# The second group's front in bunches of pieces behind each quartet of sums, instead of one piece behind every fetch

## The reference, cut to what matters

```python
h = rms_norm(x, norm1_gain) * (1 + scale1) + shift1
z = h @ w_in                                   # q, k, v, conv inputs, merge gates
y_att = attend(q, k, v) @ w_o_att              # banded attention, 8 heads x 64
y_conv = (cb * conv_y) @ w_o_conv              # short convolution
mixed = (sigmoid(ga) * y_att + sigmoid(gb) * y_conv) @ w_o
x = x + gate1 * mixed
h2 = rms_norm(x, norm2_gain) * (1 + scale2) + shift2
# PEER: for each frame, 8 heads pick the top 16 of 128 x 128 experts
u = take(expert_u, idx); act = gelu(einsum("thkd,td->thk", u, h2))
out = einsum("thk,thkd->td", softmax(top) * act, take(expert_v, idx))
x = x + gate2 * out
```

## Time and profile before

| | |
|---|---|
| Time, median of 3 runs | 2077.7 us (2077.1 to 2078.39) |
| The profiled execution | 2079.57 us, its span 2077.4 us |
| PE busy over the span | 1690.4 us (81%) |
| DVE busy | 1221.6 us (59%) |
| ACT busy | 724.9 us (35%) |
| Indirect gathers | 604.02 MB, 71.3% of the time of the 16 DMA engines |
| Mean granted TensorE clock | 0.957 of full speed |

### The profile page before, as it was taken

One profiled execution on the slowest core, in us unless ns is written; L12 is line 12 of the kernel. 1 busy time (PEld: TensorE's weight loads), 2 busy tenths in 40 slices (PEclk: granted clock), 3 DMA queues, 4 the chain that ended last, 5 costly groups with the idle time before them and its releaser, 6 DMA issues.

```text
span 2077.4 us, 22509 instructions
## 1 busy us (share of the span) xinstructions
PE 1690.4 (81%) x7500; PEld 771.4 (37%) x7500; DVE 1221.6 (59%) x3212; ACT 724.9 (35%) x2231; POOL 607.4 (29%) x584
## 2 busy tenths in 40 slices
PE   6999997669978799989967777777777777777776
PEld 3864896435445455445522121121121121121111
DVE  3334116866565454447867777777677675555554
ACT  3125103442475223232343333333333343333332
POOL 0000001332322223222254434434444434333331
PEclk8999999779977999999999999999999999999999
DMA  9546514889965799967799999999999999999995
GB/s 400 212 173 255 221 52 167 341 336 385 358 235 199 315 400 370 421 254 276 269 373 422 421 421 422 421 421 421 421 421 421 422 421 422 421 422 421 421 421 240
DMA packets 102467, 718.50 MB, mean 346 GB/s; under 512 B 13584, under 2 KB 13584, under 8 KB 15696
## 3 DMA queue, kind: packets, MB, share of 16 engines
q0 software_dynamic: 82944, 604.02, 71.3%
q1 hardware_dynamic: 18544, 110.69, 13.6%
q10 hardware_dynamic: 864, 2.36, 0.3%
HBM read 712.30 MB, written 4.73 MB: 345 GB/s over the span
## 4 chain that ended last, share of the span: by engine, by line
DMA 41%; PE 30%; DVE 14%; issue 10%; ACT 4%; POOL 1%; SPq 0%; DVEq 0%; POOLq 0%; ACTq 0%
DMA ring<-in_expert_uv_dram,uidx 40%; PE ps L564 7%; PE ps L825 6%; PE ps L683 5%; DVE ring L1492 5%; PE ps L689 2%; PE ps L704 2%; POOL ring L437 1%; PE ps L560 1%; DMA ring<-in_wpack_dram 1%; PE ps L627 1%; PE ps L594 1%; PE ps L534 1%; ACT wdiag L1088 1%; DVE left L1393 1%
## 5 line engine op out<-in xcount | busy, mean ns | idle before, releaser
L825 PE MATMUL ps<-ring,wdiag 128*32 128x512 f32 x2304 | 866.6, 635 | 246.8 <-ACT wdiag L1088 228.0
L437 POOL DMA_INDIRECT ring<-in_expert_uv_dram,uidx x576 | 606.1, 1052 | 1387.0 <-PE ps L825 959.8
L1492 DVE CUSTOM_DVE_ANT_0 ring<-ring,mA 128x1024 f32<-128x1024 f32 x576 | 700.4, 1223 | 427.8 <-DMA ring<-in_expert_uv_dram,uidx 422.0
L825 PEld LDWEIGHTS ps<-ring,wdiag 128*32 128x32 f32 x2304 | 174.0, 114 | 881.0 <-ACT wdiag L1088 552.4
L1081 ACT ACTIVATE gel<-act_in 128x1 f32<-128x1 f32 x576 | 116.7, 203 | 875.5 <-DVE act_in L1492 875.0
L1088 ACT ACTIVATE wdiag<-repeat,wsel 128x32 f32<-128x32 f32 x576 | 185.1, 321 | 18.8
L1083 ACT ACTIVATE wsel<-gel,gsel 128x1 f32<-128x1 f32 x576 | 169.7, 295 | 18.7
L564 PE MATMUL ps<-hB,ring 128*128 128x384 f32 x320 | 109.3, 493 | 0.0
L745 PE MATMUL ps<-hB,ring 128*128 128x384 f32 x256 | 89.4, 504 | 8.5 <-issue 8.5
L683 PE MATMUL ps<-hB,ring 128*128 128x384 f32 x256 | 87.9, 498 | 9.8 <-DVE kv L1317 9.8
L564 PEld LDWEIGHTS ps<-hB,ring 128*128 128x128 f32 x320 | 59.0, 190 | 42.5 <-issue 6.3
(11 more groups left out here) (238 smaller groups left out, 1611.7 us busy)
## 6 DMA issues: line engine op xcount, KB each, us to landing
ring<-in_wpack_dram SPq DMA_DIRECT2D x96, 1024.0 KB, 8.9
ring<-in_expert_uv_dram,uidx POOLq DMA_INDIRECT x576, 22.7
xB<-in_x_b_dram SPq DMA_DIRECT2D x2, 1536.0 KB, 20.3
o_y_p<-mA ACTq DMA_DIRECT2D x16, 128.0 KB, 5.2
bias<-in_bias_dram SPq DMA_DIRECT2D x1, 1024.0 KB, 32.2
o_v_p<-kv SPq DMA_DIRECT2D x4, 256.0 KB, 11.1
o_k_p<-xB SPq DMA_DIRECT2D x4, 256.0 KB, 10.0
xB<-in_keysT_dram SPq DMA_DIRECT2D x1, 1024.0 KB, 9.6
```

The costliest lines, as they stand in the source:

```text
L437: nc.gpsimd.indirect_dma_start(out=ring[:, slot, :], out_offset=None, in_=ins["expert_uv"], in_offset=bass.IndirectOffsetOnAxis(ap=uidx[:, ...
L825: mm = nc.tensor.matmul(pY[c * GT:(c + 1) * GT, half, :], wdiag[:, n % NDIAG, :], ring[:, ROW[n][0], D + half * 512:D + (half + 1) * 512], ...
L1492: nc.vector.tensor_tensor_reduce(r, r, h2n[:, g % 2, :], 1.0, 0.0, ALU.mult, ALU.add, act_in[:, g % 2, j:j + 1]).then_inc(s["dot"], 1)
```

## The change

The loop condition in `order()` alone is changed (REP = 4, RUN = 28, PLACE_AT[2] = 180):

```diff
     for n in range(RUN, EARLY):
         out.append(("gather", n))
         if n == PLACE_AT[1]:
             out.append(("place", 1))
-        while done < len(left) and done * (PLACE_AT[2] - 8 - RUN) < (n + 1 - RUN) * len(left):
+        while n % REP == 1 and done < len(left) and done * (PLACE_AT[2] - 8 - RUN) < (n + REP - RUN) * len(left):
             out.append((1, left[done]))
             done += 1
         if n == PLACE_AT[2]:
             out.append(("place", 2))
```

## The result

The changed kernel takes 2204.98 us (median of 4 runs, 2203.73 to 2207.38), the kernel before 2078.05 beside it (4 runs): the ratio is 1.061, 95% interval 1.0592 to 1.0628. The forecast was 2280 us, the range 2190 to 2350. The profiled execution took 2203.73 us, its span 2201.2.

A forecast was written before the change was run, and what follows sets the result against it. Before the full-DMA tail, PE paces the gathers, so each us of new PE waiting adds one at the end. 30 + 15 + 46 + 14 + 48 + 50 = 203 us on 2079.57, adjusted to the median: 2280 us, range 2190 to 2350.

The forecast's parts named there:

- the clock's term: Outside attention: some 25 new PE waits of 2 us or more, each followed by low clock, 2 us each: 50 us.
- The cover of the quartets: Before each quartet: PE loses two pieces (5.2 us) of cover and waits 140 to 150 us for diagonals instead of 2.5.
- rival A: Whole kernel faster, about 2053 us: attention's chain freed of dots and tables, quartets still covered; chance 0.04.
- Projection 29 of 30: Bunches 29 to 49 (six): PE waits at their ends and behind two moved pieces, 30 us longer.
- merge 39 of 46: Bunches 81 to 121 (eleven): PE waits set by each bunch's last piece, 46 us longer.
- output projection and norm 12 of 14: Bunches 125 to 137 (four): PE waits at their ends and a later first routing piece, 14 us longer.
- Attention 3.8 of 15: Bunches 53 to 77 (seven): ends cost 35 us, fewer waits and gaps give some back, net 15 us longer.
- Routing 40 of 48: Bunches 141 to 169 (eight): quartets wait behind a head's search on DVE, 48 us longer.
- The formula: In routing: PE's wait is 13.6 us less 2.62 us per piece standing behind the key scores in the bunch.
- Rival C: Whole stretch runs at attention's mean clock of 0.75: +152 us instead of +50, 2382 us; chance 0.08.
- B: Short bunch ends vanish in slack; only routing, norm and long chains remain: about +70, 2148 us; chance 0.10.
- D: Whole kernel: nothing changes, since PE's order is the same and DVE and ACT would have room; chance 0.02.

The follow-up runs named there:

- e4_whole: Changed kernel with one more PE wait: each quartet waits for its last diagonal before its first fold; 2257.63 us, ratio 1.0816.
- e10_late_quartet: Changed kernel with only PE's quartets of gathers 29 to 169 moved two pieces later into the bunch (one unit in attention); 2112.2 us, ratio 1.0172.
- e7_tanh_before: Kernel before with tanh in place of gelu, so attention needs one table only; ratio 0.9991.
- e6_at_only: Kernel before with only attention's units in bunches behind n % 4 = 1; ratio 1.0042.
- e5_rt_only: Kernel before with only the routing's pieces in bunches behind n % 4 = 1; ratio 1.0212.
- e2_behind3: Changed kernel with its bunches behind gathers with n % 4 = 3 instead of 1; ratio 1.0109.

## Why the prediction was right, and its one wrong term

**The total.** 2205 lies inside the range of 2190 to 2350, near its low end, which had put nothing on the clock. The point, 2280, is 75 us too high: 50 of it is the clock's term, the rest attention, merge, routing and norm. Without that term it would have been 2230.

**What bounds it: right.** A us that PE loses in the stretch is a us at the end. The five stages and the 5.8 us behind them sum to the 124 us by which the span grew, and the tail kept its 421 GB/s.

**The cover of the quartets: right, mechanism and size.** PE's waits for diagonals were put at 140 to 150 us; measured 163.6, though only 61.0 of it shows as idle time. By its letter the test that I had named (wrong if PE waits less than 100 us for `wdiag`) fails at 60.7 us. The test was badly put, since waiting between single folds counts as busy: e4_whole, where it can't, shows 166.2. Single bunches come out as computed: the one of gather 113, with its exponential, at 6.0 (6.0 computed); one in the merge that ends on a piece with a tanh takes 4.87 us for its quartet, 2.9 over the earlier trace rows (3.15 computed). e10_late_quartet shows it as the cause: with two pieces of PE put back between dot and fold, and nothing else, 91 of 127 us are gone. The sum has small slips that change nothing: the earlier trace rows give 15.01 us from key scores to fold, not 15.05, and rival A's 2053 is 25 below the median of 2077.7, not below 2079.6.

**Projection 29 of 30, merge 39 of 46, output projection and norm 12 of 14: right.** In the merge the folds alone hold PE 42.2 us more. In the norm the folds hold PE 22.5 us more, but the wait of 8.54 us ahead of the first routing piece is nearly gone (0.7): the two waits overlap, which makes 12.

**Attention 3.8 of 15.** Its sum was ends of 35, less 17 elsewhere, less a little clock. Measured: the folds 27.6 more, the rest 20 less (idle 24.9 to 15.3, busy 78.0 to 67.9), and some 4 us more of it runs beside the folds. PE's waits at L611 shrank by 8.4 us (12 computed), but not through the table loads: these went from 12 to 6, and e7_tanh_before shows them to be worth nothing. Nor is it the order of dots and spreads alone: e10_late_quartet has that order to the letter, and its waits at L611 are 17.6 us. Part of the waiting has only moved to the folds, where PE now stands while DVE and ACT catch up. Of the 10 us of busy time, e4_whole loses 6.5 again with the clock at 0.71 there instead of 0.89, so they belong to the clock, and it was luck: with the same bunches e6_at_only has a clock of 0.78 and loses 11.9 us.

**Routing 40 of 48.** The formula held at the bunches that were looked at, and e5_rt_only gives 44. What was too much is the sum: I added the waits of all bunches and took off nothing for the busy time that comes back (111.3 to 104.5 us beside the folds). 5.2 of these are the low clock of L745 and L725 in the kernel before, behind waits that the change removes (89.4 to 85.6, 14.2 to 12.8).

**The clock, about 0 of 50: wrong, and this is the term that failed.** The step was that a wait of 2 us or more of PE at the bunch's end puts the following instructions at the low level, as the earlier trace rows show behind waits of 9.77 and 8.54 us. Those waits are in one piece. Here the diagonals come one after another, each releases a fold, and each lone fold holds PE for up to 1.90 us. So the wait of 6 us at gather 113 holds 1.86 us of idle time. The busy time of L683 and L745 (87.0 and 85.6 us; 87.9 and 89.4 before) shows no surcharge, which is the test I had named; the other sign, a mean clock below 0.93, did not come either. A surcharge is there all the same, but small and inside the folds, which stand first behind a wait: 4.77 us for eight instructions behind 7.91 us, 3.23 for a lone fold (1.90 elsewhere) behind 3.68. Outside attention PE is busy 33 us of the time at the lower level, 30 of them in folds (13 and none in the kernel before). Half of that is lost, so some 10 us more than before (an estimate from the clock's records); attention gives about as much back. Rival C falls with it. e4_whole is the kernel that I had priced: 166 us of waits in one piece each, the low level behind them, and 1.0816.

**Rivals A, B, D: wrong.** A asked for bunch ends under 1.3 us on average; they are 4.5 (163.6 over 36 bunches). B asked for the short ends to vanish in slack; the projection and the merge alone give 68 us. D is contradicted by the result.

**Left open**: what e2_behind3 still loses in attention and merge, and what e10_late_quartet still loses in attention, norm and routing.

## What to carry to other kernels

When in-order queues share one list, ask of each consumer how much of its own work lies between the producer's last instruction and the consumer's use of it; here that was two pieces of PE (5.2 us), and a reordering that changed nothing on PE cost 6% by taking it away. Move the consumer as well as the producers (a quartet two pieces later gave back 91 of 127 us), and try a lump at each position of the period before judging it (1.061, 1.038, 1.011, 1.029). Price waits by whether they are broken: many short waits with work between them cost little more than their length, the same time in one piece costs the clock behind it too. And read a mean over stages last: the clock's 0.94 here was a gain in one stage over a loss in others.

## What the runs showed of the hardware

- A lone fold (4 instructions, 128x512, one 32-column strip of PE) takes 1.90 us and four folds on four strips 1.95 us. Busy time of such instructions can therefore double with no more work done: 98.7 to 203.8 us in this stretch. A group whose count and mean duration are the same (592 and 661 ns, 595 and 667 ns before) and whose busy time has doubled is a hidden wait.
- The granted clock was 0.94 over a stretch with 164 us of waits broken by lone folds, and 0.85 with 166 us of waits in one piece each, the work being the same.
- Twelve table loads of 1.283 us with their way back in 120 us of attention cost nothing that can be measured. Two of them between the last pieces and a quartet cost 2.8 us of PE's time (7.95 and 5.1 us).
